# HGRN output transposed in the third gate product's slot, v transposed beside the diagonal, and four other reorderings in a one-core decoder step

## The chip, the cores and the metric

The kernel runs on one core of one Trainium2 chip (trn2). The metric is the time of one launch in microseconds of device time: 2454.43 us in the median of three runs (2454.26 to 2455.49). The engines are TensorE (PE, matmuls; PEld is its weight load), VectorE (DVE), ScalarE (ACT), GpSimd (POOL) and SyncE (SP, which only issues DMAs).

## The reference, cut to what matters

One decoder layer over 2096 tokens of width 1024: 16 meta tokens and 2048 prompt tokens as one sequence, and 8 running sequences of 4 tokens ("the tail").

```python
u = rmsnorm(x) @ w_in                      # 1024 -> 3072: xa, ga, q, f, i (=v), gb
# RG-LRU group, 4 blocks of 128 channels
xc = conv4(xa);  r = sigmoid(xc @ w_ra);  ig = sigmoid(xc @ w_rx)
a  = exp(-8 * r * softplus(-lam));  h = scan(a, sqrt(1 - a*a) * ig * xc)
y_a = h * gelu(ga)
# HGRN2 group, 4 heads of 128 keys x 128 values, in chunks
f = lb + (1 - lb) * sigmoid(f);  k = (1 - lb) * sigmoid(-f_pre);  q = silu(q) / sqrt(128)
o = (q * decay) @ S + tril(q k^T with decay) @ v;   S = S * decay + (k * decay)^T @ v
o = rms(o) * gn * silu(gb)
x = x + concat(y_a, o) @ w_out
x = x + relu(rmsnorm(x) @ w_up)**2 @ w_down          # 1024 -> 4096 -> 1024
y = rmsnorm(x) * ln_final
```

The outputs are y and the states after the last token. All is fp32.

## The kernel before

Activations lie transposed (channels on partitions, tokens along the free axis). The tokens are worked on in two passes: p = 0 has 1024 tokens in two tiles of 512, p = 1 has the other 1072 (the tail among them) in three tiles of 358, 358 and 356. Every dense product is made of three matmuls: weights and activations are each split into a rounded part (`w_hi`, `a_hi`, made by ACT) and a remainder (`w_lo`, `a_lo`), and hi*hi, hi*lo and lo*hi are summed in PSUM (L476 to L478). A unit is one block of 128 output channels for one tile: 8 k-blocks by 3, so 24 matmuls into one of four PSUM banks. There are 96 weight blocks: 24 of the input projection, 8 of the output projection (from `OUT0` = 24), 64 of the MLP. Pass 0 rounds them, makes the remainders and writes both to HBM (`kept_hi`, `kept_lo`); pass 1 only reads them back (`reload`, on POOL's queue), a block when the block two before is done.

The remainder `w_lo` of a weight block is made by `split`. Of pass 0's blocks POOL does 0 and 1, DVE 2 to 23, and POOL all from 24 on.

The order around the change is written out by hand in `schedule(p)`. The input projection has four iterations of five blocks (V, G, XA, F, Q for head i and for RG-LRU block i) and a fifth with the four GA blocks. A block has a slot for each half unit (4 k-blocks, 12 matmuls): 20 slots in an iteration of pass 0, 30 in one of pass 1. All engines walk the same list. Behind the half unit of a slot, PE does the pieces that the list has there; each other engine does its share of the unit (after the second half) and then its share of the pieces, in program order. The pieces of head i-1 run in iteration i: VT (PE transposes v, 9 tiles in pass 1), D (q k^T of 32x32 diagonal blocks), L1 to L7 (the levels above), KT, U (state updates), O (the output), R and N (its norm: DVE inverts the roots, ACT scales), OT (PE transposes the scaled output), Y (DVE multiplies by the gate). GATE(i) is the RG-LRU gate products of block i (4 or 6 matmuls, ACT's sigmoids behind them); GA and GB are the rest of RG-LRU, GB with the scan. Four further PSUM banks (`aux`) are handed round in the list's order; who opens one waits for the reader of the one four before.

Two waits of DVE matter below. It writes v of a new head over the old one:

```python
if kind == V and it > 0:
    filled(dve, AUX[(p, "VT", it - 1)] + 1 + p)
```

that is, `read_out` of a V unit waits until PE has transposed the last tile of the head before. And DVE does GB of block i-1 behind the first V unit (slot 0 in pass 0, slot 1 in pass 1), and in D it multiplies q by f (L1197), on which L1 waits on PE.

The output projection begins with `SIDE` = 4 units side by side, each first for the six k-blocks that are ready early (`EARLY`), then for the last two. Pass 0's final norm is worked in pass 1's first iteration: NF (PE sums squares), FN (DVE's reciprocals), FY (eight scalings and stores). At the end of pass 1 the last two output blocks are taken tile by tile (`FINAL_ORDER`), so that the final norm of a tile (sum on PE, root on ACT, reciprocal and eight scalings on DVE in `finish_tile`, stores on SP) can begin before the last unit.

Of the kernel before, what the change touches and what calls it, by code (L numbers as in the profile page):

```python
# [31 lines left out]
KB = DM // P  # L32
# [27 lines left out]
GA0, OUT0, MLP0 = 20, 24, 32  # L60
OUT_ORDER = [0, 1, 2, 4, 5, 6, 7, 3]
EARLY = 6
SIDE = 4


PC = {}
# [18 lines left out]
def y_no(p, t, n):  # L85
# [4 lines left out]

FINAL_ORDER = [[(m, t) for m in range(KB) for t in range(NT[0])],
               [(m, t) for m in range(KB - 2) for t in range(NT[1])]
               + [(m, t) for t in range(NT[1]) for m in (KB - 2, KB - 1)]]
FINAL_AT = [{mt: n for n, mt in enumerate(order)} for order in FINAL_ORDER]


# [34 lines left out]
def s_at(p, i, name):  # L131
# [3 lines left out]

PREP_STEPS = 25
PIECES = ["VT", "D"] + [f"L{l}" for l in range(1, 8)] + ["KT", "U", "O", "R", "N", "OT", "Y"]
SLOTS = [dict(zip(range(16), PIECES)),
         dict(zip([0, 4, 5, 6, 8, 9, 10, 12, 13, 14, 15, 16, 18, 19, 21, 22], PIECES))]
GATE_SLOT = [16, 24]  # L140
GATE_A_SLOT, GATE_B_SLOT = [18, 27], [0, 1]

SQUARES_AFTER = {1: [0], 2: [1], 3: [2], 4: [3], 5: [4, 5], 6: [6, 7]}
RS_SLOT = [7, 1]

FINAL_SLOTS = {6: ("NF", 0), 7: ("FN", 0), 8: ("FN", 1), **{10 + b: ("FY", b) for b in range(8)}}
TURN_SLOTS = [{14: 0}, {20: 0, 22: 1}]


def schedule(p):  # L150

    out = []
    for i in range(HEADS + 1):
        blks = [5 * i + b for b in range(5)] if i < HEADS else [GA0 + c for c in range(4)]
        s = 0
        for blk in blks:
            for t in range(NT[p]):
                for half in range(2):
                    pieces = []
                    if p and i == 0 and s in FINAL_SLOTS:  # L160
                        pieces.append(FINAL_SLOTS[s])
                    if i == 0 and s == RS_SLOT[p]:
                        pieces.append(("RS", 0))
                    if i >= 1 and s in SLOTS[p]:
                        pieces.append((SLOTS[p][s], i - 1))
                    if i < HEADS and s == GATE_SLOT[p]:
                        pieces.append(("GATE", i))
                    if i < HEADS and s == GATE_A_SLOT[p]:
                        pieces.append(("GA", i))
                    if i >= 1 and s == GATE_B_SLOT[p]:  # L170
# [41 lines left out]
def build(nc, ins, outs):  # L212
# [6 lines left out]
    with ExitStack() as ctx:  # L219
# [200 lines left out]
        @block.gpsimd  # L420
        def _(pool):
            pool.memset(ones[:, :], 1.0).then_inc(consts, 1)
            pool.memset(eps[:, :], EPS).then_inc(consts, 1)
            pool.memset(hprev[:, :], 0.0).then_inc(consts, 1)
            pool.memset(xhist[:, :, :], 0.0).then_inc(consts, 1)
            pool.memset(state[:, :, :], 0.0).then_inc(consts, 1)

            def split(slot, n):

                pool.wait_ge(w_split, n + 1)  # L430
                pool.tensor_tensor(w_lo[:, slot, :], w_st[:, slot, :], w_hi[:, slot, :].bitcast(F32),  # L431
                                   ALU.subtract).then_inc(w_ready, 1)

            pool.wait_ge(consts, 1)
            for j in range(2):
                split(j, j)
            pool.wait_ge(w_ready, OUT0)
            with pool.Fori(OUT0 // 2, BLOCKS // 2) as i:
                for j in range(2):
                    split(j, 2 * i + j)  # L440

            def reload(m, slot):
                pool.dma_start(w_hi[:, slot, :], kept_hi[m]).then_inc(w_again[slot], 16)  # L443
                pool.dma_start(w_lo[:, slot, :], kept_lo[m]).then_inc(w_again[slot], 16)

            pool.wait_ge(w_ready, BLOCKS)
            pool.memset(q_seq[:, :, :], 0.0).then_inc(q_spread, 1)
            for j in range(2):
                pool.wait_ge(w_kept[j], 32 * (BLOCKS // 2))
                pool.wait_ge(unit_done, unit_no(0, BLOCKS + j - 1, 0))  # L450
                reload(j, j)
            with pool.Fori(1, BLOCKS // 2) as i:
                for j in range(2):
                    pool.wait_ge(unit_done, 2 * NT[1] * i + unit_no(1, j - 1, 0))
                    reload(2 * i + j, j)
# [3 lines left out]
        def _(pe):  # L459
# [165 lines left out]
            for p in range(2):  # L625
# [18 lines left out]
                             y_ready if m == 0 else None, lambda j: y_no(p, t, j))  # L644

                units = [(m, t) for m in range(KB) for t in range(nt)]
                for m, t in units[:SIDE]:
                    if t == 0:
                        weights(p, OUT0 + m)
                    open_unit(unit_no(p, OUT0 + m, t))  # L650
                    out_unit(m, t, range(EARLY))
                for m, t in units[:SIDE]:
                    out_unit(m, t, range(EARLY, KB))
                for m, t in units[SIDE:]:
                    if t == 0:
                        weights(p, OUT0 + m)
                    open_unit(unit_no(p, OUT0 + m, t))
# [54 lines left out]
            for m, t in FINAL_ORDER[1][-2 * NT[1]:]:  # L712
# [1 line left out]
                    mlp_weights(last, 1, 1, m - 4)  # L714
                unit = mlp_unit(last, 1, 1, m - 4, t, FINAL_AT[1][(m, t)] - 4 * NT[1])
                products(*unit, halves(0))
                if t and m == KB - 2:
                    final_sum(1, t - 1)
                products(*unit, halves(1))
            final_sum(1, NT[1] - 1)  # L720

# [2 lines left out]
        def _(act):  # L724
# [94 lines left out]
            def piece(p, name, i):  # L819
# [50 lines left out]
                elif name == "O":  # L870
# [9 lines left out]
                    if p:  # L880
                        fn(o_ss[0:T8, 8:9], o_ss[0:T8, 8:9], ACT.Sqrt, bias=eps[0:T8, 0:1], scale=1.0 / P)
                    fn(o_ss[:, 0:NCH], o_ss[:, 0:NCH], ACT.Sqrt, bias=eps[:, 0:1],
                       scale=1.0 / P).then_inc(o_sums, 1)
                    if p and i + 1 < HEADS:
                        act.wait_ge(s_step, s_at(p, i, "smul"))
                        load_state(i + 1)
                    if p:
                        for s in (3, 4):
                            drained(act, AUX[(p, "U", i)] + s)
                        act.dma_start(ssn_d[i], tmp[:, :, :]).then_inc(s_store, 16)  # L890
                elif name == "N":
# [64 lines left out]
            for p in range(2):  # L956
# [42 lines left out]
                    drained(act, AUX[(1, "U", 3)] + 2)  # L999
                    act.dma_start(sp_d, state[:, :, :]).then_inc(small_out, 16)  # L1000

                turn(p, NT[p] - 1, range(EARLY))
                if p == 0:
                    round_weights(OUT0 + 1)
                for t in range(NT[p]):
                    turn(p, t, range(EARLY, KB))

# [55 lines left out]
                for m, t in FINAL_ORDER[p]:  # L1063
# [11 lines left out]
                    if p == 0 and (m, t) == (KB - 1, 0):  # L1075
                        act.wait_ge(unit_done, unit_no(0, BLOCKS - 1, 0) + 1)
                        round_x(1, 0)
                    if p and t and m == KB - 2:
                        rms_tile(1, AUX[(1, "NF", 0)], rf, t - 1, KEPT)
            rms_tile(1, AUX[(1, "NF", 0)], rf, NT[1] - 1, KEPT)  # L1080

            act.wait_ge(s_store, 16 * HEADS)
# [4 lines left out]
        def _(dve):  # L1087
# [310 lines left out]
            for p in range(2):  # L1398
# [13 lines left out]
                queue = []  # L1412
                started = False
                for it, blk, t, half, pieces in schedule(p):
                    if p == 0 and 0 < blk < OUT0 - 1 and t == 0 and half == 0:
                        n = blk + 1
                        dve.wait_ge(w_ready, n)
                        dve.wait_ge(w_split, n + 1)
# [111 lines left out]

            for m, t in FINAL_ORDER[1]:
                last_sum(m, t)
                if t and m == KB - 2:
                    finish_tile(t - 1, range(3))
                elif t and m == KB - 1:
                    finish_tile(t - 1, range(3, KB))
            finish_tile(NT[1] - 1, range(KB))


# [92 lines left out]
```

## Time and profile before

| | us |
|---|---|
| median of the runs | 2454.43 |
| the profiled execution's own time | 2457.05 |
| its span | 2455.2 |
| PE busy | 2393.2 |
| DVE, ACT, POOL busy | 940.7, 643.8, 287.6 |
| mean granted clock of TensorE | 0.989 |

Times in rows are microseconds from the span's start. In the view of the instructions in order of time a row has start, length, engine, line, operation, out<-in, and in brackets the idle time of that engine just before and what ended it. In the table by stretches the fields behind the colon are the stretch's length, busy time and count of instructions for each engine, the granted clock of TensorE (1.00 is 2.4 GHz, 0.50 is 1.2 GHz), the DMA engines' share and GB/s.

### The profile page before, as it was taken

Reading aid. Unit: us, or ns where it says so; the run is one execution under the profiler, and the core shown is the slowest. Engines: PE = TensorE matmul, PEld = TensorE weight load, DVE = VectorE, ACT = ScalarE, POOL = GpSimd, SP = SyncE. Lnnn points to the kernel's source line nnn. Section 1 sums busy time; section 2 is a strip of 40 time slices with the busy share of each in tenths; the row PEclk is TensorE's granted clock in tenths of the full one; section 3 lists DMA queues with packets and bytes.
Section 4 is the critical chain, followed back from the end, with each engine's and each line's share of the span. In section 5 each row is a group of like instructions: output and inputs, shape, how many; then the busy total and the mean of one; then the engine's idle time right before and its main releaser. Section 6 shows DMA issues by size and latency. Waiting matters only on the chain.

```text
span 2455.2 us, 38591 instructions
## 1 busy us (share of the span) xinstructions
PE 2393.2 (97%) x15842; PEld 2148.2 (87%) x15842; DVE 940.7 (38%) x1593; ACT 643.8 (26%) x1199; POOL 287.6 (12%) x276
## 2 busy tenths in 40 slices
PE   7999998999999999999999999999999999999997
PEld 5777786888888888888898899999999999999996
DVE  6766564421121121223765566544212211211224
ACT  5345343331131121223334234422201201200211
POOL 0000002222122122222000000010000100000000
PEclk9999998999999999999999999999999999999998
DMA  5332325444444434454422222332222232223223
GB/s 199 108 114 97 109 91 176 137 156 143 151 133 149 153 130 153 144 201 145 138 96 69 70 70 87 98 136 91 90 86 86 88 100 86 85 85 93 95 86 106
DMA packets 88162, 284.39 MB, mean 116 GB/s; under 512 B 15856, under 2 KB 19056, under 8 KB 88048
## 3 DMA queue, kind: packets, MB, share of 16 engines
q1 hardware_dynamic: 46512, 158.09, 19.0%
q0 software_dynamic: 27648, 100.68, 12.7%
q10 hardware_dynamic: 13888, 23.95, 2.9%
q8 instruction: 90, 1.47, 0.2%
q14 instruction: 24, 0.20, 0.0%
HBM read 171.07 MB, written 111.62 MB: 115 GB/s over the span
## 4 chain that ended last, share of the span: by engine, by line
PE 88%; DVE 6%; issue 3%; ACT 2%; ACTq 1%; DMA 0%; POOL 0%; DVEq 0%; POOLq 0%
PE bank L476 28%; PE bank L478 27%; PE bank L477 27%; PE aux L617 1%; PE aux L543 1%; DVE a_lo L1178 1%; DVE xc L1361 1%; PE aux L571 1%; ACT s_in L726 1%; PE aux L594 1%; PE aux L593 1%; PE aux L548 0%; DVE xy L1287 0%; DVE rs L1122 0%; DVE xy L1113 0%
## 5 line engine op out<-in xcount | busy, mean ns | idle before, releaser
L476 PE MATMUL bank<-a_hi,w_hi 128*128 128x358 f32 (+3 forms) x2560 | 923.8, 361 | 31.1 <-DVE a_lo L1178 11.4
L477 PE MATMUL bank<-a_lo,w_hi 128*128 128x358 f32 (+3 forms) x2560 | 906.7, 354 | 0.0
L478 PE MATMUL bank<-a_hi,w_lo 128*128 128x358 f32 (+3 forms) x2560 | 906.6, 354 | 0.0
L476 PEld LDWEIGHTS bank<-a_hi,w_hi 128*128 128x128 f32 x2560 | 485.8, 190 | 82.6 <-POOL w_lo L431 19.3
L478 PEld LDWEIGHTS bank<-a_hi,w_lo 128*128 128x128 f32 x2560 | 486.5, 190 | 43.6
L477 PEld LDWEIGHTS bank<-a_lo,w_hi 128*128 128x128 f32 x2560 | 486.4, 190 | 42.9 <-issue 1.5
L476 PE MATMUL bank<-b_hi,w_hi 128*128 128x358 f32 (+3 forms) x1280 | 450.2, 352 | 0.0
L477 PE MATMUL bank<-b_lo,w_hi 128*128 128x358 f32 (+3 forms) x1280 | 449.1, 351 | 0.0
L478 PE MATMUL bank<-b_hi,w_lo 128*128 128x358 f32 (+3 forms) x1280 | 449.1, 351 | 0.0
L1489 DVE TENSOR_TENSOR xy<-xy,bank 128x356 f32 (+6 forms) x160 | 94.1, 588 | 554.9 <-PE bank L478 554.9
L726 ACT ACTIVATE a_hi<-tmp 128x356 f32 (+5 forms) x160 | 88.3, 552 | 817.3 <-DVE tmp L1479 817.3
L431 POOL TENSOR_TENSOR w_lo<-w_st,w_hi 128x1024 fp32r<-128x1024 f32 x74 | 183.8, 2484 | 975.4 <-ACT w_hi L726 975.4
L478 PEld LDWEIGHTS bank<-b_hi,w_lo 128*128 128x128 f32 x1280 | 240.8, 188 | 20.6
L477 PEld LDWEIGHTS bank<-b_lo,w_hi 128*128 128x128 f32 x1280 | 240.4, 188 | 20.7 <-issue 0.2
L476 PEld LDWEIGHTS bank<-b_hi,w_hi 128*128 128x128 f32 x1280 | 240.2, 188 | 19.9 <-issue 0.2
L1479 DVE SCALAR_TENSOR_TENSOR tmp<-bank,rs 128x356 f32<-128x356 f32 (+2 forms) x160 | 94.6, 591 | 332.1 <-PE bank L478 331.1
L443 POOL DMA_DIRECT2D w_hi<-kept_hi x96 | 51.2, 534 | 1144.1 <-PE bank L478 1144.1
L726 ACT ACTIVATE w_hi<-w_st 128x1024 fp32r<-128x1024 f32 x96 | 100.9, 1051 | 276.0 <-PE bank L478 272.9
L1482 DVE TENSOR_TENSOR a_lo<-tmp,a_hi 128x356 f32 (+5 forms) x160 | 95.2, 595 | 197.9 <-ACT tmp L726 197.9
L726 ACT ACTIVATE tmp<-tmp 128x356 f32<-128x356 f32 (+2 forms) x160 | 85.7, 535 | 0.0
L726 ACT ACTIVATE tmp<-xy 128x496 f32<-128x496 f32 (+2 forms) x75 | 40.8, 545 | 146.2 <-DVE xy L1489 146.2
L726 ACT ACT_TABLE_LOAD x57 | 73.1, 1283 | 6.9 <-issue 5.9
(162 smaller groups left out, 1417.3 us busy)
## 6 DMA issues: line engine op xcount, KB each, us to landing
w_st<-in_wall SPq DMA_DIRECT2D x96, 512.0 KB, 4.1
kept_hi<-w_hi SPq DMA_DIRECT2D x96, 512.0 KB, 4.9
kept_lo<-w_lo SPq DMA_DIRECT2D x96, 512.0 KB, 5.7
w_hi<-kept_hi POOLq DMA_DIRECT2D x96, 512.0 KB, 4.0
w_lo<-kept_lo POOLq DMA_DIRECT2D x96, 512.0 KB, 4.7
xs<-in_xT ACTq DMA_DIRECT2D x8, 536.0 KB, 7.5
xy<-in_xT ACTq DMA_DIRECT2D x8, 536.0 KB, 8.3
xy<-in_xT ACTq DMA_DIRECT2D x8, 512.0 KB, 7.7
```

The costliest lines, as they stand in the source:

```text
L431: pool.tensor_tensor(w_lo[:, slot, :], w_st[:, slot, :], w_hi[:, slot, :].bitcast(F32), ALU.subtract).then_inc(w_ready, 1)
L443: pool.dma_start(w_hi[:, slot, :], kept_hi[m]).then_inc(w_again[slot], 16)
L476: pe.matmul(ps, wh, xh, start=(j == 0), stop=False)
L477: pe.matmul(ps, wh, xl, start=False, stop=False)
L478: mm = pe.matmul(ps, wl, xh, start=False, stop=(j == 7))
L543: mm = pe.matmul(ps[s0:s0 + w, HALF * c:HALF * (c + 1)], k[:, at:at + w], right_halves(q, at, w, x), start=True, stop=True)
L571: mm = pe.matmul(ps[:, j * P:(j + 1) * P], k_tok[0:r_, c + j, :], v_tok[0:r_, c + j, :], start=True, stop=True)
L593: pe.matmul(out, q[:, lo_:hi_], s_in[:, c + j, :], start=True, stop=False)
L726: return nc.scalar.activation(out, in_, func, **kw)
L1479: stt(z, bank[lu % 4][:, 0:w], 0.0, rs[:, c0:c0 + w], ALU.max, ALU.mult).then_inc(bank_free[lu % 4], 1)
L1482: tt(a_lo[:, 4 * qd + j, c0:c0 + w], z, a_hi[:, 4 * qd + j, c0:c0 + w].bitcast(F32), ALU.subtract).then_inc(h_ready, 1)
L1489: tt(x, x, bank[lu % 4][:, 0:w], ALU.add).then_inc(bank_free[lu % 4], 1)
```

## The change

Nothing is computed otherwise; order and engines change.

1. `AT`: the slots of the pieces. VT goes from slot 0 to slot 1 in pass 0 and from slot 0 to slot 4 in pass 1, so that it stands right ahead of D. GATE(i) goes one slot ahead (16 to 15, 24 to 23), and OT and Y of head i-1 go into that slot, ahead of it. In the fifth iteration (`AT_LAST`, no GATE) OT and Y keep slots 14 and 15 in pass 0 and get 22 and 23 in pass 1.
2. FN, FY and NF of pass 0 go three slots back (NF from slot 6 to 9, FN to 10 and 11, FY to 13 to 20).
3. The remainders of blocks 2, 3 and 4 are made by POOL and no longer by DVE (`DVE_FIRST` = 5).
4. Output projection of pass 0: three units side by side in place of four, and ACT rounds block 25 ahead of the second tile's `turn`, no longer behind it.
5. ACT's load of the next state and its store of the last one go from behind O to behind N.
6. The last six units of pass 1 are reordered, with the sums and `finish_tile`.

```diff
-SIDE = 4
+SIDE = [3, 4]
+DVE_FIRST = 5
@@
-               + [(m, t) for t in range(NT[1]) for m in (KB - 2, KB - 1)]]
+               + [(KB - 2, 0), (KB - 2, 1), (KB - 1, 0), (KB - 1, 1), (KB - 2, 2), (KB - 1, 2)]]
+SUM_AT = {(KB - 1, 1): 0, (KB - 2, 2): 1}
@@
-SLOTS = [dict(zip(range(16), PIECES)),
-         dict(zip([0, 4, 5, 6, 8, 9, 10, 12, 13, 14, 15, 16, 18, 19, 21, 22], PIECES))]
-GATE_SLOT = [16, 24]
+AT = [[1] + list(range(1, 14)) + [15, 15],
+      [4, 4, 5, 6, 8, 9, 10, 12, 13, 14, 15, 16, 18, 19, 23, 23]]
+AT_LAST = [AT[0][:-2] + [14, 15], AT[1][:-2] + [22, 23]]
+GATE_SLOT = [15, 23]
@@
-FINAL_SLOTS = {6: ("NF", 0), 7: ("FN", 0), 8: ("FN", 1), **{10 + b: ("FY", b) for b in range(8)}}
+FINAL_SLOTS = {9: ("NF", 0), 10: ("FN", 0), 11: ("FN", 1), **{13 + b: ("FY", b) for b in range(8)}}
@@ schedule
-                    if i >= 1 and s in SLOTS[p]:
-                        pieces.append((SLOTS[p][s], i - 1))
+                    if i >= 1:
+                        at = (AT if i < HEADS else AT_LAST)[p]
+                        pieces += [(name, i - 1) for name, slot in zip(PIECES, at) if slot == s]
@@ gpsimd
-            for j in range(2):
-                split(j, j)
+            for n in range(DVE_FIRST):
+                split(n % 2, n)
@@ tensor
-                for m, t in units[:SIDE]:
+                for m, t in units[:SIDE[p]]:
...
-                if t and m == KB - 2:
-                    final_sum(1, t - 1)
+                if (m, t) in SUM_AT:
+                    final_sum(1, SUM_AT[(m, t)])
@@ scalar: "O" -> behind "N"
-                    if p and i + 1 < HEADS:
-                        act.wait_ge(s_step, s_at(p, i, "smul"))
-                        load_state(i + 1)
-                    if p:
-                        for s in (3, 4):
-                            drained(act, AUX[(p, "U", i)] + s)
-                        act.dma_start(ssn_d[i], tmp[:, :, :]).then_inc(s_store, 16)
...
-                turn(p, NT[p] - 1, range(EARLY))
                 if p == 0:
                     round_weights(OUT0 + 1)
+                turn(p, NT[p] - 1, range(EARLY))
@@ vector
-                    if p == 0 and 0 < blk < OUT0 - 1 and t == 0 and half == 0:
+                    if p == 0 and DVE_FIRST - 1 <= blk < OUT0 - 1 and t == 0 and half == 0:
...
-                if t and m == KB - 2:
-                    finish_tile(t - 1, range(3))
-                elif t and m == KB - 1:
-                    finish_tile(t - 1, range(3, KB))
+                if (m, t) == (KB - 1, 1):
+                    finish_tile(0, range(5))
+                elif (m, t) == (KB - 2, 2):
+                    finish_tile(0, range(5, KB))
+            finish_tile(1, range(KB))
             finish_tile(NT[1] - 1, range(KB))
```

## Rows read from the trace of the kernel before

**Rows 1.** The page: busy time and share of each engine.
```profile
PE 2393.2 (97%) x15842; PEld 2148.2 (87%) x15842; DVE 940.7 (38%) x1593; ACT 643.8 (26%) x1199; POOL 287.6 (12%) x276
```
**Rows 2.** The table by stretches, two of dense products, one in each pass.
```profile
500.00:525.00 25.00, 25.00 (x112) 20.70 (x111) 6.16 (x9) 8.54 (x13) 5.82 (x3) 1.00 0.53 183
...
2000.00:2300.00 300.00, 300.00 (x1837) 300.00 (x1836) 60.38 (x114) 33.49 (x75) 26.45 (x50) 1.00 0.28 90
```
**Rows 3.** The same table, behind three waits of PE.
```profile
407.00:413.00 6.00, 5.68 (x14) 4.59 (x15) 3.33 (x5) 2.19 (x3) 1.99 (x2) 0.50 0.73 249
...
1314.00:1321.00 7.00, 6.62 (x26) 5.96 (x24) 1.68 (x3) 1.67 (x6) 0.00 (x0) 0.52 0.01 2
...
1492.00:1499.00 7.00, 6.62 (x42) 6.16 (x42) 2.80 (x6) 2.39 (x9) 0.52 (x1) 1.00 0.00 0
```
**Rows 4.** Instructions in order of time, DVE, pass 1, iteration 1, slots 1 to 4.
```profile
1253.77 0.53 DVE L1321 TENSOR_TENSOR v<-bank,rs 128x358 f32<-128x358 f32 x1 [1.17 <-PE bank L478]
...
1260.32 1.28 DVE L1197 TENSOR_TENSOR q<-q,f 128x1072 f32<-128x1072 f32 x1 [0.42 <-PE aux L530]
```
**Rows 5.** The same view, PE: where D and L1 begin.
```profile
1259.48 0.31 PE L530 MATMUL aux<-q,k 128*32 128x32 f32 x13
...
1262.33 0.45 PE L543 MATMUL aux<-q,k 128*32 128x16 f32 x32
```
**Rows 6.** Chain that ended last: start, length, what; N on ACT, GATE on PE.
```profile
1312.51 2.17 ACT s_in L726 x8
...
1324.46 3.60 PE aux L617 x12
```
**Rows 7.** Instructions in order of time: OT on PE, Y on DVE.
```profile
1313.69 0.33 PE L608 MATMUL aux<-ident,s_in 128*128 128x128 f32 x1 [1.96 <-ACT s_in L726]
...
1314.45 0.75 DVE L1263 SCALAR_TENSOR_TENSOR xy<-aux,par,gate 128x512 f32<-128x512 f32 x1 [0.77 <-PE aux L608]
```
**Rows 8.** The same view, output projection of pass 0: ACT, DVE, POOL, PE.
```profile
376.28 3.22 ACT L726 ACTIVATE a_hi<-xy 128x512 fp32r<-128x512 f32 x6
...
378.33 6.07 DVE L1170 TENSOR_TENSOR a_lo<-xy,a_hi 128x512 fp32r<-128x512 f32 x10
...
399.33 0.67 DVE L1459 TENSOR_TENSOR xy<-xy,bank 128x496 f32<-128x496 f32 x1 [14.93 <-PE bank L478]
...
380.52 6.07 POOL L431 TENSOR_TENSOR w_lo<-w_st,w_hi 128x1024 fp32r<-128x1024 f32 x1 [12.43 <-ACT w_hi L726]
...
386.65 0.78 PE L476 MATMUL bank<-a_hi,w_hi 128*128 128x496 f32 x1 [3.08 <-POOL w_lo L431]
...
407.32 0.78 PE L476 MATMUL bank<-a_hi,w_hi 128*128 128x496 f32 x1 [4.00 <-POOL w_lo L431]
```
**Rows 9.** The same view, start of pass 1: NF's second sum on PE, DVE's first reciprocal.
```profile
1196.49 2.04 PE L493 MATMUL aux<-gate,ones 128*128 128x512 f32 x2 [4.77 <-ACT rs L726]
...
1197.48 2.39 DVE L1103 RECIPROCAL rs<-rs 128x358 f32<-128x358 f32 x1 [10.04 <-DMA spad<-in_conv]
```
**Rows 10.** The same view, pass 0: DVE beside POOL, and iteration 0.
```profile
406.55 1.25 DVE L1461 SCALAR_TENSOR_TENSOR b_lo<-xy,par,b_hi 128x496 fp32r<-128x496 f32 x1 [1.28 <-ACT tmp L726]
...
69.92 1.28 DVE L1321 TENSOR_TENSOR f<-bank,rs 128x512 f32<-128x512 f32 x2
...
79.36 0.69 DVE L1321 TENSOR_TENSOR q<-bank,rs 128x512 f32<-128x512 f32 x1 [4.25 <-PE bank L478]
...
70.06 0.50 PE L476 MATMUL bank<-a_hi,w_hi 128*128 128x512 f32 x1 [2.00 <-DVE w_lo L1419]
...
248.00 0.28 PE L543 MATMUL aux<-q,k 128*32 128x16 f32 x11 [0.62 <-DVE q L1197]
```
**Rows 11.** The same view, the end: the last weight, DVE's last sum and scalings.
```profile
2416.41 0.43 PE L476 MATMUL bank<-a_hi,w_hi 128*128 128x358 f32 x1 [3.60 <-DMA w_lo<-kept_lo]
...
2443.33 0.53 DVE L1512 TENSOR_TENSOR gate<-gate,tmp 128x356 f32<-128x356 f32 x1 [0.56 <-ACT tmp L726]
...
2448.70 4.09 DVE L1113 SCALAR_TENSOR_TENSOR xy<-xy,par,gate 128x356 f32<-128x356 f32 x8
```

More of the change, by code:

```diff
@@ L651, in _ @@
                     out_unit(m, t, range(EARLY))
-                for m, t in units[:SIDE]:
+                for m, t in units[:SIDE[p]]:
                     out_unit(m, t, range(EARLY, KB))
-                for m, t in units[SIDE:]:
+                for m, t in units[SIDE[p]:]:
                     if t == 0:
@@ L899, in piece @@
                         ins.then_inc(aux_free[(ao + s) % 4], 1)
+                    if p and i + 1 < HEADS:
+                        act.wait_ge(s_step, s_at(p, i, "smul"))
+                        load_state(i + 1)
+                    if p:
+                        for s in (3, 4):
+                            drained(act, AUX[(p, "U", i)] + s)
+                        act.dma_start(ssn_d[i], tmp[:, :, :]).then_inc(s_store, 16)
                 elif name == "TURN":
@@ L1077, in _ @@
                         round_x(1, 0)
-                    if p and t and m == KB - 2:
-                        rms_tile(1, AUX[(1, "NF", 0)], rf, t - 1, KEPT)
+                    if p and (m, t) in SUM_AT:
+                        rms_tile(1, AUX[(1, "NF", 0)], rf, SUM_AT[(m, t)], KEPT)
             rms_tile(1, AUX[(1, "NF", 0)], rf, NT[1] - 1, KEPT)
```

## The prediction

> **What bounds the kernel now.** The page comes first: PE is busy 97% of the span, DVE 38% [rows 1]. So an edit counts only by what it does to PE's idle time and clock, and to the tail behind PE's last product. The table by stretches gives PE's pace: 0.223 us a product in pass 0 (25 us by 112), 0.163 in pass 1 (300 by 1837) [rows 2]; a half unit of 12 is 2.7 and 1.96 us, a unit twice that. Then the waits of PE in the order of time [rows 7 to 11]: 2.00 at 70 us, 3.08 and 4.00 in the output projection of pass 0, 4.77 at the start of pass 1, 1.96 for OT, 3.60 for the last weight. Last the same table behind such waits [rows 3]: the clock is at 0.50 (the 1.2 GHz level) for the 6 us behind the wait of 4.00, at 0.52 for 7 us behind that of 1.96, and at 1.00 behind the same OT wait two heads later. So a drop costs about half of its 6 to 7 us, 3 us, and a wait near 2 us may or may not bring it. I take 2.7 for a drop where part of it passes in the wait itself.
>
> All sums are made on the profiled execution: 2457.05 us, span 2455.2, which is 2.6 over the median of the runs (2454.43). I carry the difference over to the median.
>
> **VT beside D in pass 1: a new wait, +14.4 and +8.1 us.** PE's own work ahead of L1 is the same in both orders. But DVE's first V read of a new head, in slot 1, waits for VT of the old one, and VT is now behind slot 4. Queued behind that read on DVE are GB with its scan, the second V read, then q times f in D, and PE waits for that in L1. The row of q times f and that of the first V read give the length of this queue: 1260.32 - 1253.77 less 0.42 idle is 6.1 us, and 1.28 for the product, 7.4 us [rows 4]. VT's last tile is done about when D began, 1259.48, and some 0.3 us pass until DVE sees it: 1259.8 + 7.4 = 1267.2 in place of 1262.33 [rows 5], so 4.8 us. Nothing hides it: PE has D alone and one half unit (2.0 us) between VT and L1. It comes in iterations 1, 2 and 3 (the fifth reads no V): 14.4 us. Each of these waits is longer than the 4.00 us one that brought the clock down [rows 3, 8], so three drops of 2.7, 8.1 us. Bounds: no drops at 14.4, three full ones at 24.9. In pass 0 VT goes back one slot only and DVE reaches that V read later than VT ends: nothing.
>
> **OT and GATE in one slot, pass 1: -9.9 us.** ACT's scaling N of eight tiles begins at 1312.51 and lasts 2.2 us [rows 6]; PE stands 1.96 us for its first tiles [rows 7]. Two half units later (3.9 us) N is over. From the half unit ahead of OT (1311.7, where the idle 1.96 begins) to the first product behind GATE (1324.46 + 3.60 = 1328.1, less 0.4 overlap: 1327.6 [rows 6]) it was 15.9 us with a drop. Anew: three half units 5.9, OT 1.1, GATE 3.4, and a new wait inside. GATE's second product needs the aux bank that Y of OT's first four tiles frees, and DVE is still at the last F tile and the three steps of the one before, about 1.9 us from the slot's end, then Y with 0.75 [rows 7]: PE stands 0.9. Sum 11.3 with 0.2 of changes between kinds of product: 4.4 less. Heads 0 and 1 alike; head 2 had no drop [rows 3]: 1.4. Together 10.2; ACT's two DMA issues now stand in front of the last F tile, so I take 9.9. Bounds: 5 if OT, the new wait and GATE bring a drop of their own, 11.
>
> **The same in pass 0: -0.2 us.** OT's wait goes there too (about 0.9 us a head), but L1 waits for DVE's q times f, idle 0.62 [rows 10], and DVE's chain to it begins with a remainder that now waits until ACT is through with GATE. PE is earlier by 0.8 and DVE by 0.05, so PE waits longer at L1. Bounds: -2.5 and +1.5.
>
> **Remainders 2 to 4 on POOL: +2.2 and +2.3 us.** DVE is spared three products of about 1.23. The first lets the reciprocals start 0.6 earlier, worth 0.3 at the low clock. The third falls on the convolution of block 0. A DVE step with two SBUF inputs beside POOL's product takes 1.25 us in place of 0.73 [rows 10]: it stands until POOL is done. POOL's product is 2.4 us, so the first two-input tap ends 2.1 us late, DVE reads F at 70.5 and no longer at 69.92, and behind it ACT does F, now GATE too (five steps and a table load, 6 us), and only then rounds block 5, whose remainder stands ahead of DVE's read of Q: 81.6 for 79.36 [rows 10]. L1 follows by the same 2.2. PE no longer waits 2.00 at 70.06 [rows 10], does GATE one slot sooner, and so stands 3.7 us more at L1: a drop, 2.7 with a chance of 0.85, 2.3. Bounds: -1 (DVE is not held) and +6.
>
> The Trainium skill has a rule on this, in GPSIMD Engine Reference, section Key points: the engine shares its SBUF interfaces with VectorE and contends with instructions in a two-port mode or with two SBUF inputs. The trace agrees (1.25 for 0.73, and POOL's own product 6.07 us beside a run of such steps [rows 8]); without that rule the edit would be a gain of about 1 us.
>
> **Output projection of pass 0: -12.0 us.** Block 25 is rounded at 376.3, where `turn` began, and no longer behind it [rows 8]; POOL's product starts at 377.4, ahead of DVE's run of a_lo at 378.33, and ends at 379.8 where it was 386.6. The run is held to 380.3: PE waits 1.6 at the second tile. Three early parts end at 388.5 (18 products each), the late parts of the first two at 389.9 and 391.2, of the third at 392.6; then unit (1,1) with 24 products to 398.2. The first unit's end leads to remainder 26: before, 399.33 (DVE's read) to 407.3 [rows 8], 8.0 us; now 390.1 to 398.1. So (2,0) starts at 398.2 where it was 407.32: 9.1. The drop behind 407 goes, 2.9 [rows 3]. Bounds: -8.5 if POOL loses to DVE as at 380.52, -12.5.
>
> **Start of pass 1: +4.9 us.** PE's wait at NF, 4.77, hid NF and one half unit under a wait that stays: unit 4 needs the bank of the first V tile, read by DVE at 1197.48 + 2.39 + 0.53 = 1200.4, and that start hangs on a small DMA [rows 4, 9]. With NF three slots later PE runs dry at 1192.7, goes on at 1200.5 and does NF's 1.8 us in the open: 2.5 us late by slot 10, the low clock taken alike. Then the scalings FY stand behind the convolution, three of 1.2 us more than before, so the last F tile is read at 1238.7 while GATE starts at 1235.8; its fifth product waits for ACT's first sigmoid, 2.1 us. With 0.3 of shifts 4.9. Bounds: 1 and 7.
>
> **The end: -2.9 us.** With (6,1) between (6,0) and (7,0) the last weight has a unit more to land: the wait of 3.60 and its low clock go. But of tile 1 all stays for the end. Behind DVE's last sum (2443.33) were five scalings, a reciprocal and eight (2448.70 + 4.09) [rows 11]: 9.5 us. Now two reciprocals of 2.39 [rows 9] and sixteen scalings of 0.51, 13.0, behind a last sum at 2436.9 (PE is done at 2434.3, DVE has three scalings of tile 0 ahead): 2449.9. Bounds: -4.5 and 0.
>
> **Small ones: -0.4 us,** for four joined stretches of transposes in pass 1. ACT's later DMAs have room (the state is needed a head later).
>
> Sum: 14.4 + 8.1 - 9.9 - 0.2 + 4.5 - 12.0 + 4.9 - 2.9 - 0.4 = +6.5. 2457.05 + 6.5 = 2463.5 for the profiled kind of execution, and 2460.9 for the median.
>
> **The rivals.** (a) The waits are there but bring no new drops: -8.1 - 2.3, so 2450.5. For it: 1.00 behind the third OT wait [rows 3]; against it, these waits are twice as long. (b) The wait for VT doesn't reach PE, since DVE's queue behind V is shorter than PE's work to L1 or is made up later: -22.5, 2438. Against it: 7.4 us stand against 2.9. This is the way in which the change would plainly gain. (c) POOL starves in the output projection as at 380.52 and the gain there is 8.5: 2464.4. (d) OT, the wait for Y and GATE together bring a drop in each of three heads: +8, 2469. [...]
>
> **How the numbers follow.** A measurement of this kernel tells some 0.2% (4.9 us) from no change. Forecast 0.55, with its own range 2456 to 2466; (a) 0.14; (b) 0.06; (c) 0.14; (d) 0.11. Faster: (b) and a quarter of (a), with a little for gains that I priced low, 0.12. Slower, above 2459.3: seven tenths of the forecast, most of (c) and all of (d), 0.63. Within: 0.25. The range takes (a) and (d): 2449 to 2470.
>
> **What would show it.** In pass 1, iterations 1 to 3: PE idle 4.8 us ahead of L1 (L543), released by L1197, clock 0.5 behind it, and the first V read beginning behind L520. OT (L608) with no wait; 0.9 ahead of GATE's second product. Pass 0: (2,0) some 9 us earlier against its stage's start, POOL's product of block 25 at 2.4 us; a tap of the convolution at 3.4 us or so where it was 1.28; L1 at 97.7. Pass 1: NF with no wait, an idle time of 7.8 us ahead of slot 8. The end: thirteen us from the last sum to the last scaling. If L1's wait in pass 1 is below 3 us, or no drop follows, the forecast is wrong in its sign.

## The result, and the profile after

The changed kernel takes 2458.85 us in the median of 20 runs (2457.79 to 2461.25), the kernel before 2455.18 in 20 runs beside them (2453.61 to 2458.73): a ratio of 1.0015 [1.0009, 1.0021], 3.7 us slower (2.2 to 5.2 by the interval), where 6.5 were forecast. That is less than the 4.9 us which the forecast gave as the least that a measurement tells from no change; with 20 runs of each kernel it is clear of the noise. The profiled execution took 2460.49, its span is 2458.3 (before: 2457.05 and 2455.2), the mean granted clock 0.989 in both. Line numbers behind L422 are four higher than before.

The page says nothing of where the time went: each engine is as busy as in [rows 1].

```profile
PE 2387.6 (97%) x15842; PEld 2145.5 (87%) x15842; DVE 939.7 (38%) x1590; ACT 646.0 (26%) x1201; POOL 291.6 (12%) x279
```

The waits of PE by what ended them do (total us, times, longest).

```profile
PE aux L547 <- DVE q L1201: 21.2, 7, 4.5
PE bank L480 <- DVE v L1325: 13.5, 2, 7.9
...
PE aux L621 <- ACT ta L730: 1.4, 1, 1.4
PE aux L621 <- DVE xy L1267: 1.3, 3, 0.4
```

The first row is L1 waiting for q times f: seven waits with 21.2 us. The wait of OT (L612) is gone in pass 1, and three of 0.4 for Y stand inside GATE (L621). What answers to [rows 4] and [rows 5], on PE and on DVE, in order of time:

```profile
1265.74 1.05 PE L547 MATMUL aux<-q,k 128*32 128x16 f32 x64 [4.54 <-DVE q L1201]
```
```profile
1258.38 0.53 DVE L1325 TENSOR_TENSOR v<-bank,rs 128x358 f32<-128x358 f32 x1 [6.99 <-PE aux L524]
1258.83 1.26 DVE L1282 TENSOR_TENSOR k_tok<-k_tok,ea 128x1072 f32<-128x1072 f32 x1
...
1260.68 2.45 DVE L1291 TENSOR_TENSOR_SCAN xy<-ta,hprev,k_tok 128x1072 f32<-128x1072 f32 x1
...
1263.97 0.53 DVE L1325 TENSOR_TENSOR v<-bank,rs 128x358 f32<-128x358 f32 x1
1264.42 1.27 DVE L1201 TENSOR_TENSOR q<-q,f 128x1072 f32<-128x1072 f32 x1
```

DVE stands 6.99 us for VT (L524), then does its whole queue, and q times f ends at 1265.7, when L1 starts. From the start of the V read it is 7.3 us, where I had 7.4. The table by stretches shows the clock behind the three such waits (to be read as [rows 3]):

```profile
1263.70:1270.50 6.80, 4.76 (x80) 4.52 (x80) 5.64 (x14) 0.00 (x0) 0.00 (x0) 0.50 0.37 127
...
1355.80:1362.70 6.90, 6.00 (x148) 5.56 (x148) 4.57 (x11) 0.00 (x0) 0.00 (x0) 0.51 0.21 77
1448.00:1451.40 3.40, 3.33 (x76) 3.29 (x76) 3.17 (x9) 0.00 (x0) 0.00 (x0) 0.50 0.15 53
```

Two times the 1.2 GHz level lasts 6.8 us, the third time 3.4, behind waits of one length (4.54, 4.55, 4.54). OT, the wait for Y and GATE in one slot, PE, against [rows 6] and [rows 7]:

```profile
1320.95 1.22 PE L612 MATMUL aux<-ident,s_in 128*128 128x128 f32 x9
1322.10 0.87 PE L621 MATMUL aux<-xc,w_ra 128*128 128x358 f32 x2
1323.39 0.87 PE L621 MATMUL aux<-xc,w_rx 128*128 128x358 f32 x2 [0.42 <-DVE xy L1267]
```

Behind them the clock stays at 1.00. Elsewhere, also in order of time: in pass 0 the first tap of the convolution beside POOL's product of block 4, and iteration 1's L1; in the output projection POOL's product of block 25 and PE's wait; the start of pass 1 on PE; the end on DVE.

```profile
57.97 2.87 POOL L435 TENSOR_TENSOR w_lo<-w_st,w_hi 128x1024 fp32r<-128x1024 f32 x1 [6.16 <-ACT w_hi L730]
...
58.60 4.64 DVE L1365 SCALAR_TENSOR_TENSOR xc<-xpad,par,xc 128x1024 f32<-128x1024 f32 x2
...
80.33 1.22 DVE L1423 TENSOR_TENSOR w_lo<-w_st,w_hi 128x1024 fp32r<-128x1024 f32 x1 [6.59 <-ACT w_hi L730]
...
97.60 1.06 PE L547 MATMUL aux<-q,k 128*32 128x16 f32 x64 [3.52 <-DVE q L1201]
...
382.44 2.38 POOL L435 TENSOR_TENSOR w_lo<-w_st,w_hi 128x1024 fp32r<-128x1024 f32 x1 [9.30 <-ACT w_hi L730]
...
385.51 0.47 PE L480 MATMUL bank<-a_hi,w_hi 128*128 128x512 f32 x1 [2.03 <-DVE a_lo L1174]
...
1195.85 0.67 PE L480 MATMUL bank<-a_hi,w_hi 128*128 128x358 f32 x1 [7.92 <-DVE v L1325]
...
1234.29 0.87 PE L621 MATMUL aux<-xc,w_ra 128*128 128x356 f32 x2 [1.35 <-ACT ta L730]
...
2442.51 0.53 DVE L1516 TENSOR_TENSOR gate<-gate,tmp 128x356 f32<-128x356 f32 x1 [0.57 <-ACT tmp L730]
...
2451.80 4.09 DVE L1117 SCALAR_TENSOR_TENSOR xy<-xy,par,gate 128x356 f32<-128x356 f32 x8
```

The same event of PE in both traces, one under the other, gives what each stage cost. "Forecast" is the term of the prediction.

| stretch, to the event | before | after | stage | forecast |
|---|---|---|---|---|
| pass 0 to OT of iteration 4 | 370.05 | 375.09 | +5.0 | +4.3 |
| to the MLP's norm sums, pass 0 | 480.82 | 475.90 | -10.0 | -12.0 |
| to slot 25 of pass 1, iteration 0 | 1238.49 | 1237.3 | +3.7 | +4.9 |
| three times V read, VT, D, L1 | | | +13.8, and +5.9 by the clock | +14.4, +8.1 |
| three times OT, Y, GATE | | | -11.5 | -9.9 |
| to the norm sums of pass 1 | 1680.89 | 1687.49 | -0.4 | -0.4 |
| to the end of the span | 2455.2 | 2458.3 | -3.5 | -2.9 |

For the pass 1 rows, L1 of iteration 1 moves from 1262.33 to 1265.74, of iteration 2 from 1351.43 to 1356.70, of 3 from 1440.61 to 1448.07, and slot 25 of the three iterations from 1327.63, 1416.77, 1502.97 to 1328.26, 1419.65, 1509.94. (In the changed kernel slot 25 is taken as the end of GATE and one half unit of 1.98 us.) From slot 25 to the next L1 it takes 4.6 us more each time, which is the wait. From L1 to slot 25 it takes 2.8, 2.4 and 0.5 less, and that holds two things, the low clock and OT with GATE. Experiment 1 separates them: it has the same list from L1 on, and its clock isn't low there. From L1 to OT it takes 53.17, 53.18 and 53.18 us, the changed kernel 55.21, 55.64 and 54.56. So the low clock costs 2.0, 2.5 and 1.4 us, and OT with GATE gives 4.8, 4.9 and 1.9.

### The profile page after: what moved, and what is told of

Same layout as the page of the kernel before. It is cut to its first block, busy times and chain, and to the rows that moved or that the text cites. A ratio compares the mean times of both kernels' runs of the same rounds, so it can differ in the third digit from the quotient of the medians.

```text
span 2458.3 us, 38591 instructions
## 1 busy us (share of the span) xinstructions
PE 2387.6 (97%) x15842; PEld 2145.5 (87%) x15842; DVE 939.7 (38%) x1590; ACT 646.0 (26%) x1201; POOL 291.6 (12%) x279
## 4 chain that ended last, share of the span: by engine, by line
PE 88%; DVE 6%; ACT 2%; issue 1%; DMA 1%; ACTq 0%; DVEq 0%; POOL 0%; POOLq 0%
PE bank L480 28%; PE bank L482 27%; PE bank L481 27%; PE aux L547 1%; PE aux L621 1%; DVE xy L1291 1%; DVE xy L1117 1%; PE aux L575 1%; PE aux L598 1%; PE aux L597 1%; PE aux L552 1%; DVE a_lo L1182 0%; ACT L730 0%; DVE q L1201 0%; DVE k_tok L1282 0%
```

## Experiments

Runs of the kernel before beside them had medians of 2454.90 us (9 runs, experiments 1 to 4), 2455.89 (21 runs, 5 to 8) and 2455.74 (11 runs, 9 to 11). Two edits have no run of their own: VT one slot later in pass 0, and ACT's two DMAs behind N.

**1. VT back in slot 0 in pass 1.** The changed kernel with one number changed.

```diff
-      [4, 4, 5, 6, 8, 9, 10, 12, 13, 14, 15, 16, 18, 19, 23, 23]]
+      [0, 4, 5, 6, 8, 9, 10, 12, 13, 14, 15, 16, 18, 19, 23, 23]]
```

> The changed kernel with one number put back: VT of pass 1 in slot 0 again (D stays in 4). Theory (DVE's V read waits for VT, GB and q times f are queued behind it): the three waits of PE ahead of L1 (4.6, 4.6 and 4.6 us in the trace of the changed kernel) and the three low-clock stretches behind them (some 2.4, 3.0 and 1.7) go: 20.8 us less than the changed kernel, about 2438, clock 1.00 through iterations 1 to 3 of pass 1. Rival 1: the low clock there comes from the stretch of small products and stays: 13.8 less, 2445. Rival 2: what PE waits for is GB itself, wherever VT stands, since GATE is now a slot sooner: less than 5 us gained, above 2453.

2439.86 us (2437.65 to 2442.03), 0.9938 [0.9924, 0.9952]: 19.0 us below the changed kernel, near the 20.8 of the theory. The V read and L1's product on DVE, and PE's waits:

```profile
1250.20 0.53 DVE L1325 TENSOR_TENSOR v<-bank,rs 128x358 f32<-128x358 f32 x1 [1.15 <-PE bank L482]
...
1256.73 1.28 DVE L1201 TENSOR_TENSOR q<-q,f 128x1072 f32<-128x1072 f32 x1 [0.41 <-PE aux L534]
```
```profile
PE aux L547 <- DVE q L1201: 7.7, 4, 3.5
```
```profile
1250.00:1540.00 290.00, 288.71 (x3402) 267.84 (x3401) 187.18 (x386) 104.09 (x242) 18.57 (x34) 1.00 0.23 74
```

The V read now waits for its own bank and q times f for D; the four waits left are pass 0's, and the clock is at 1.00 through iterations 1 to 3. So one slot number decides the change's sign.

**2. VT in slot 4 alone**, in the kernel before.

```diff
-                    if i >= 1 and s in SLOTS[p]:
+                    if p and i >= 1:
+                        pieces += [(name, i - 1) for name in PIECES if AT1[name] == s]
+                    elif i >= 1 and s in SLOTS[p]:
```
(`AT1` is the old list of pass 1 with VT at 4.)

> The kernel before with VT of pass 1 in slot 4 beside D, and nothing else of the change. Theory: three waits of 4.6 to 4.8 us ahead of L1 and a drop of the clock behind each (1.7 to 3.4 us): 20 to 24 us over before, 2475 to 2479. Rival 1 (the drops depend on the rest of the change): +14, 2469. Rival 2 (the wait only exists with GATE in slot 23): within 3 us of before.

2473.48 us (2471.97 to 2475.62), 1.0073 [1.006, 1.0087]: some 18 us, a little under what was expected.

```profile
1266.43 1.05 PE L547 MATMUL aux<-q,k 128*32 128x16 f32 x64 [4.55 <-DVE q L1201]
```
```profile
1264.90:1271.70 6.80, 5.27 (x104) 4.83 (x108) 5.20 (x12) 0.00 (x0) 0.00 (x0) 0.56 0.28 102
```

The three waits (4.55, 4.53, 4.55) make 13.6. The low clock behind them costs 2.6, 1.5 and 2.2 us, read from L1 to OT of each head against the kernel before. But in this execution the clock was low for only 3.4 us behind the waits of OT in heads 0 and 1, and for 6.8 in the kernel before [rows 3]: from OT to GATE it takes 1.8 and 1.0 us less. That is why the sum stays below 20.

**3. OT, Y and GATE in slot 23 alone**, in the kernel before.

```diff
-GATE_SLOT = [16, 24]
+GATE_SLOT = [16, 23]
...
+AT1 = [dict(zip(PIECES, [0, 4, 5, 6, 8, 9, 10, 12, 13, 14, 15, 16, 18, 19] + ends)) for ends in ([23, 23], [21, 22])]
```

> The kernel before with OT and Y of pass 1 in slot 23 together with GATE (from 21, 22 and 24) in iterations 1 to 3, GATE in 23 in iteration 0 too, and nothing else of the change. Theory: OT's waits (2.0 us, three times) go, a wait of 0.6 inside GATE comes, the two drops behind OT at 1314 and 1403 go, and iteration 0 loses about 1 at GATE's fifth product, where ACT is still at the last F tile: 11.6 less than before, 2443.6. Rival 1: the two drops come anyway, from transposes and gate products side by side: 5 less, 2450. Rival 2: what was won at OT is given back at GATE's wait for Y: within 2 us.

2444.7 us (2442.9 to 2447.21), 0.9957 [0.9943, 0.997]. No wait at OT, 0.42 inside GATE, no low clock in either head:

```profile
1315.47 1.23 PE L611 MATMUL aux<-ident,s_in 128*128 128x128 f32 x9
...
1317.92 0.87 PE L620 MATMUL aux<-xc,w_rx 128*128 128x358 f32 x2 [0.42 <-DVE xy L1266]
```
```profile
1280.00:1370.00 90.00, 89.58 (x993) 82.79 (x992) 56.67 (x116) 34.35 (x81) 5.68 (x11) 1.00 0.25 83
```

**4. Final norm of pass 0 in its old slots**, on top of experiment 1.

```diff
-FINAL_SLOTS = {9: ("NF", 0), 10: ("FN", 0), 11: ("FN", 1), **{13 + b: ("FY", b) for b in range(8)}}
+FINAL_SLOTS = {6: ("NF", 0), 7: ("FN", 0), 8: ("FN", 1), **{10 + b: ("FY", b) for b in range(8)}}
```

> As the first, and FINAL_SLOTS as before the change too (NF in slot 6, FN in 7 and 8, FY in 10 to 17). Theory (NF and one half unit are hidden by a wait that stays; behind slot 8 NF stands in the open, and FY behind the convolution makes GATE's fifth product wait): 2.5 to 3.7 less than the first kernel, 2434.5 to 2435.5. Rival: the cost at the start of pass 1 is that of GATE one slot sooner, and NF's place is worth nothing: the same as the first kernel, 2438.

2438.11 us (2437.49 to 2438.49), 1.75 below experiment 1, less than was expected and not apart from it by the intervals (0.9931 [0.9917, 0.9945] for 0.9938 [0.9924, 0.9952]); in the trace the stretch from the residual's sums to VT of iteration 1 (1172.68 to 1245.61) is 2.4 shorter (1171.66 to 1246.99 there). NF's wait is back and hides its own work, but a wait inside iteration 0's GATE stays:

```profile
1190.08 2.05 PE L497 MATMUL aux<-gate,ones 128*128 128x512 f32 x2 [4.80 <-ACT rs L730]
...
1230.56 0.86 PE L621 MATMUL aux<-xc,w_ra 128*128 128x356 f32 x2 [1.57 <-ACT ta L730]
```

With FY in its old slots GATE still starts 2.2 us ahead of DVE's read of the last F tile (1226.42 and 1228.62). Experiment 3 has the old slots too and stands 1.38 us at the same place. So this wait comes from GATE in slot 23, not from FY; experiment 11 takes it away.

**5. Remainders 2 to 4 back on DVE**, on top of experiment 1.

```diff
-DVE_FIRST = 5
+DVE_FIRST = 2
```

> The first kernel (VT of pass 1 in slot 0) with the remainders 2 to 4 on DVE again (DVE_FIRST = 2), GATE still in slot 15 of pass 0. Theory (POOL's product holds the first two-input tap of the convolution for 2.1 us, and the three products that DVE is spared are worth less): the tap takes 1.28 us, not 3.32, PE waits 2.0 for remainder 4 at 70 us again, L1 of iteration 1 begins 0.5 to 1 sooner than 97.6 and with 1 to 2 us of idle ahead of it in place of 3.5, so that the drop there goes: 2 to 4 less than the first kernel, 2436 to 2438. Rival 1 (POOL's help is worth its place, the late L1 comes from GATE alone): 1 to 2 more, 2441. Rival 2: what counts is the order on ACT and both are alike within 0.5.

2438.1 us (2436.68 to 2439.39), 0.9929 [0.9916, 0.9943]. The reason given for it fell. The hold is gone (three taps in 3.92 us), yet DVE does its own product instead, and F is read at 70.08, 0.1 sooner than in experiment 1 counted from PE's start (43.42 here, 42.78 there, F at 69.57). L1 is as late as before, with the same wait:

```profile
59.02 3.92 DVE L1365 SCALAR_TENSOR_TENSOR xc<-xpad,par,xc 128x1024 f32<-128x1024 f32 x3
...
68.94 1.23 DVE L1423 TENSOR_TENSOR w_lo<-w_st,w_hi 128x1024 fp32r<-128x1024 f32 x1
...
97.12 1.06 PE L547 MATMUL aux<-q,k 128*32 128x16 f32 x64 [3.54 <-DVE q L1201]
```

By the medians it is 1.8 us below experiment 1, again inside the intervals. So what makes L1 late is not where the remainders are made. The row of 80.33 in the changed kernel names it: DVE stood 6.59 us for ACT's rounding of block 5, and that is behind GATE's sigmoids. Experiments 8 and 10 take that up.

**6. ACT rounds block 25 ahead of the second tile's turn, alone**, in the kernel before.

```diff
-                turn(p, NT[p] - 1, range(EARLY))
                 if p == 0:
                     round_weights(OUT0 + 1)
+                turn(p, NT[p] - 1, range(EARLY))
```

> The kernel before with ACT's rounding of block 25 ahead of the second tile's turn, nothing else (four units side by side). Theory: POOL's product takes 2.4 in place of 6.07 and PE's wait of 3.08 at (1,0) falls to 0, the wait for a_lo grows from 0.7 to 2; the wait of 4.0 ahead of (2,0) stays, since remainder 26 hangs on the first unit's end: 2 to 5 less than before (a drop may go), 2450 to 2453. Rival (the order on ACT is all of the gain): 10 less, 2445.

2451.89 us (2450.73 to 2453.8), 0.9986 [0.9977, 0.9995].

```profile
377.69 2.38 POOL L431 TENSOR_TENSOR w_lo<-w_st,w_hi 128x1024 fp32r<-128x1024 f32 x1 [9.30 <-ACT w_hi L726]
...
380.77 0.47 PE L476 MATMUL bank<-a_hi,w_hi 128*128 128x512 f32 x1 [2.04 <-DVE a_lo L1170]
...
404.42 0.78 PE L476 MATMUL bank<-a_hi,w_hi 128*128 128x496 f32 x1 [4.00 <-POOL w_lo L431]
```

POOL's product is 2.38 us and not 6.07, but DVE's run of a_lo is held behind it, so PE waits 2.04 there; the wait of 4.00 stays.

**7. The end's order alone**, in the kernel before.

```diff
-               + [(m, t) for t in range(NT[1]) for m in (KB - 2, KB - 1)]]
+               + [(KB - 2, 0), (KB - 2, 1), (KB - 1, 0), (KB - 1, 1), (KB - 2, 2), (KB - 1, 2)]]
+SUM_AT = {(KB - 1, 1): 0, (KB - 2, 2): 1}
```

> The kernel before with the new order of the last six units, their sums and finish_tile, nothing else. Theory (3.6 of waiting for the last weight and its low clock go, 3.5 more of DVE work stand behind the last sum): 3 to 3.5 less than before, 2451.5. Rival 1 (the weight's wait was made up by DVE's backlog anyway): 0. Rival 2 (DVE's longer tail gives all back): 1 more.

2452.11 us (2450.09 to 2454.95), 0.9984 [0.9975, 0.9993]: 1.7 to 6.1 us by the interval, 3.8 by the medians, where the forecast's term was 2.9. The weight's wait of 3.60 [rows 11] is gone from the waits of PE.

**8. GATE in slot 16 in pass 0, OT and Y ahead of it in 15, remainder 4 on DVE**, on top of experiment 4.

```diff
-GATE_SLOT = [15, 23]
+GATE_SLOT = [16, 23]
-DVE_FIRST = 5
+DVE_FIRST = 4
```

> VT of pass 1 in slot 0, FINAL_SLOTS as before the change, and in pass 0 GATE in slot 16 again with OT and Y still in 15; POOL makes remainders 2 and 3, DVE 4. Theory (in pass 0 the gain at OT was given back at L1, since ACT's rounding for the next block, and with it DVE's remainder and its read of Q, stood behind GATE): L1 of iteration 1 near 95.2 in place of 97.6 and no drop (-4 to -5), the idle time ahead of L1 in the later iterations 0.6 and not 1.4, the period of an iteration 75.2 and not 76.1 (-2.5): 6 to 7 less than the kernel with VT and FINAL_SLOTS put back, 2431 to 2432. Rival (L1's wait in pass 0 is set by GB's scan whatever ACT does): period 76.1, only the first 4: 2434.

2428.08 us (2426.96 to 2429.51), 0.9887 [0.9872, 0.9902], better than was expected and 10.0 below experiment 4. ACT rounds block 5 at 72.26, ahead of GATE's sigmoids; in the changed kernel it does so at 79.19, behind them. L1 comes at 95.08 with an idle 0.55, and from iteration 2 to 4 it takes PE 75.04 and 75.00 us a head, where the changed kernel and the one before both need 76.0 to 76.1. What stays is

```profile
69.58 0.53 PE L480 MATMUL bank<-a_hi,w_hi 128*128 128x512 f32 x1 [1.99 <-DVE w_lo L1423]
...
95.08 0.74 PE L547 MATMUL aux<-q,k 128*32 128x16 f32 x64 [0.55 <-DVE q L1201]
...
1221.74 1.16 PE L621 MATMUL aux<-xc,w_ra 128*128 128x356 f32 x2 [1.96 <-ACT ta L730]
```
```profile
1222.20:1225.60 3.40, 3.40 (x10) 2.66 (x9) 0.00 (x0) 2.75 (x5) 0.00 (x0) 0.50 0.31 112
```

**9. Three units side by side alone**, in the kernel before.

```diff
-SIDE = 4
+SIDE = [3, 4]
```

> The kernel before with three units side by side in pass 0's output projection in place of four, and nothing else; ACT still rounds block 25 behind the second tile's turn. The change as a whole gained 10.0 us there, the rounding's order alone 3.3 (2451.9). Theory (the two gains stand apart and add up): POOL's product of block 25 is still 6.07 us and PE still waits 3.1 for it near 386.7, but the first unit is finished 4 us sooner, so the wait of 4.00 for remainder 26 and the low clock behind it (2.9) go: about 6.9 less, 2448 to 2449. Rival (the gain needs both, since the product of block 25 holds up remainder 26 too): the wait behind it stays at 2 or more, with a drop, and the time is 2453 or above.

2448.44 us (2443.25 to 2451.47), 0.9966 [0.9955, 0.9977]. POOL's product is 6.07 us still and PE waits 3.08 for it; at (2,0), where PE waited 4.00 for remainder 26, it goes on without an idle time. POOL and PE, in order of time; the last row is the first product of (2,0):

```profile
381.38 6.07 POOL L431 TENSOR_TENSOR w_lo<-w_st,w_hi 128x1024 fp32r<-128x1024 f32 x1 [12.42 <-ACT w_hi L726]
...
387.51 0.78 PE L476 MATMUL bank<-a_hi,w_hi 128*128 128x496 f32 x1 [3.08 <-POOL w_lo L431]
...
404.05 0.50 PE L476 MATMUL bank<-a_hi,w_hi 128*128 128x496 f32 x1
```

So the two edits of that stage add up: 3.4 and 8.3 us by the ratios, each with some 2.5 either way, against 10.0 in the changed kernel's trace.

**10. As 8, with remainder 4 on POOL.**

```diff
-DVE_FIRST = 4
+DVE_FIRST = 5
```

> The fastest version so far (the changed kernel with VT in slot 0 in pass 1, NF, FN and FY of pass 0 in their old slots, GATE in slot 16 in pass 0 with OT and Y in 15, remainder 4 on DVE: 2428.1 us), with the one difference that POOL makes remainder 4 too, over the convolution of block 0, as in the changed kernel. Theory (what made L1 late in pass 0 was GATE ahead of the rounding of block 5, and POOL's hold on a tap costs about what DVE's own product of 1.23 us would): L1 at about 95 in iteration 1 as with remainder 4 on DVE, F read at 70.6 or sooner, no wait of 2 us at 70, time within 1 us of 2428 (or 2 below it, if the wait near 70 was worth its length). Rival (the price that I gave for POOL's hold is real, 2.2 us and more for a drop): L1 at 97 or later with an idle time near 3, and 2430 to 2433.

2431.24 us (2430.62 to 2432.14), 0.9902 [0.9886, 0.9917]. Neither theory holds whole. The tap is held as in the changed kernel, PE doesn't wait near 70, and L1 comes 1.5 us sooner than in experiment 8, not later; but it waits 2.15 there, and the clock falls:

```profile
57.60 4.64 DVE L1365 SCALAR_TENSOR_TENSOR xc<-xpad,par,xc 128x1024 f32<-128x1024 f32 x2
...
75.85 0.69 DVE L1325 TENSOR_TENSOR q<-bank,rs 128x512 f32<-128x512 f32 x1 [1.11 <-PE bank L482]
...
93.61 0.81 PE L547 MATMUL aux<-q,k 128*32 128x16 f32 x64 [2.15 <-DVE q L1201]
```
```profile
94.00:98.00 4.00, 4.00 (x50) 3.21 (x41) 2.34 (x4) 0.00 (x0) 0.00 (x0) 0.57 0.02 9
377.00:381.00 4.00, 4.00 (x11) 3.15 (x12) 4.00 (x8) 1.90 (x4) 0.00 (x0) 0.57 0.85 207
```

Neither stretch is in experiment 8's execution, nor is a third at 1534.5, while its low clock at 1222 isn't here. The first takes most of what L1 had won: at L1 of iteration 2 only 0.2 of the 1.5 us is left (170.37 and 170.58). The profiled spans are 1.1 us apart (2428.8 and 2427.7), the medians 3.2. The mean granted clocks of all the runs point the same way: 0.992 to 0.993 in the four of this experiment, 0.994 to 0.995 in those of experiment 8. A difference of 0.002 over 2430 us is some 5 us by an estimate, rounding aside, so the low clock is enough to account for the 3.2; that nothing else has a part in it isn't shown.

This experiment differs from experiment 4 by GATE's slot in pass 0 alone. L1 comes at 93.61 for 97.19 there, and the time is 6.9 us less by the medians (0.9902 for 0.9931). What is shown is that GATE's slot makes L1 late and POOL's hold doesn't, and that the wait which goes near 70 comes back at L1.

**11. As 8, with GATE of iteration 0 of pass 1 in slot 24.**

```diff
-                    if i < HEADS and s == GATE_SLOT[p]:
+                    if i < HEADS and s == GATE_SLOT[p] + (p == 1 and i == 0):
```

> The fastest version so far (2428.1 us) with one difference: in pass 1, GATE of iteration 0 alone goes back from slot 23 to 24, where DVE and ACT have the scalings FY behind them. Theory (the wait of 1.96 at 1221.7 inside that GATE and the drop of 3.4 us behind it are worth 1.96 and 1.7, and no other wait takes their place, as iteration 0 has no OT): 2424 to 2425.5. Rival (the wait moves on to L1 of iteration 1, because ACT's gates are a slot later): 2427 to 2429.

2426.48 us (2425.78 to 2427.11), 0.9881 [0.9866, 0.9896], the fastest: 29 us below the kernel before, 32 below the changed one. The stage is shorter by what was expected (from the second NF sum to VT of iteration 1 it is 53.4 us, 57.05 in experiment 8), and the clock holds:

```profile
1222.44 0.87 PE L621 MATMUL aux<-xc,w_ra 128*128 128x356 f32 x2
```
```profile
1200.00:1280.00 80.00, 80.00 (x885) 74.70 (x884) 60.27 (x114) 23.22 (x43) 5.29 (x10) 1.00 0.36 119
```

The profiled spans are 3.2 us apart, the medians only 1.6, between the two theories. In this execution the clock fell behind PE's wait of 1.99 near 69 us, where it had not in experiment 8's; and experiment 8's profiled execution was the slowest of its four. The mean granted clocks of the four runs are alike in both (0.994 or 0.995), which fits a gain of the wait of 1.96 alone. But with four runs each 1.6 us is not separated from 3.6 with certainty. No new wait at L1 was found (the four together are 2.3 us, 2.4 in experiment 8).

## Why the prediction was right, and where its sizes were off

The mechanism was right, and the range and the sign. The sum of the table is +5.0 - 10.0 + 3.7 + 13.8 + 5.9 - 11.5 - 0.4 - 3.5 = +3.0, the span says +3.1, the forecast +6.5. Part of that is luck: the terms were too low by 2.7 us together and too high by 6.2, and what was left is 3.5. The median is also below the 2459.3 from which the forecast called it slower (0.63); it fell into the band of no change, which had 0.25.

- **VT beside D, +14.4 and +8.1: shown.** Idle 4.54 at each L1 for 4.8, with DVE's V read behind VT as its releaser; experiment 2 shows it alone (4.55), experiment 1 without (19.0 us). The three drops came, one of them half as long, and cost 5.9 us: 2.7 each was too much.
- **OT and GATE in one slot, -9.9: too small, measured -11.5.** Per head it is 4.8, 4.9 and 1.9 for 4.4, 4.4 and 1.4. The 0.5 of each is the wait for Y, 0.42 where I reckoned 0.9: Y began at 1322.60, which is 0.25 sooner, and GATE's first product lay over more of it. The 0.3 that I took off for ACT's DMAs did not show. No low clock followed in any of the three heads, so rival (d) fell. Experiment 3 alone gives 10.6 us by its ratio [7.4, 14.0]; in its trace it is 11.7 from L1 of iteration 1 to L1 of iteration 4, less the 1.38 of iteration 0.
- **Output projection, -12.0: -10.0.** POOL's product began where I had it (382.44 is the 377.4 of the forecast and the 5.0 of pass 0) and took 2.38 for 6.07. But PE waited 2.03 and not 1.6, and the clock was low behind it for 3.4 us:

```profile
386.40:389.90 3.50, 3.50 (x10) 2.72 (x9) 3.50 (x7) 1.13 (x3) 0.00 (x0) 0.51 0.89 233
```

  I had counted no drop for this wait, though it is as long as that of [rows 7], behind which the clock fell in one head and held in another.
- **Remainders on POOL, +4.5: +5.0, the right time with its cause half wrong.** Each step is in the trace: the tap of 3.3 us (I said 3.4), F at 70.55 (70.5), Q at 81.48 (81.6), L1 at 97.60 (97.7), a drop. But I booked the late rounding of block 5 on the remainders' account, and it is GATE's: with GATE in slot 16 and the same remainders on POOL (experiment 10) Q is read at 75.85 and L1 comes at 93.61. POOL's hold costs about what DVE's own product costs (experiment 5). And the -0.2 for OT and GATE in pass 0 hid a gain of 1 us a head: from iteration 2 on L1 comes every 75.0 us in experiments 8 and 10, every 76.1 with GATE in slot 15.
- **Start of pass 1, +4.9: +3.7.** The idle time behind NF's removal was 7.92 (I said 7.8), that inside GATE 1.35 where I had 2.1. For the second wait I blamed the scalings FY behind the convolution, and that was wrong: it is as long with FY in the old slots (experiments 3 and 4) and goes with GATE in slot 24 (experiment 11).
- **The end, -2.9: -3.5,** with 12.9 us from the last sum to the last scaling (13.0).
- **Rivals.** (a) no drops: fell. (b) the wait does not reach PE: fell; its price of 2438 is nearly what experiment 1 gives by really taking the wait away. (c) POOL starves: fell, 2.38 us.

The Trainium skill states, in SBUF — State Buffer, section Who interferes with whom, that a DVE instruction with two SBUF inputs contends with a GpSimd instruction that reads SBUF, and, in section SBUF: two separate sides, that whichever starts first has the shared ports for its whole instruction while the other is blocked. The trace agrees both ways: POOL began at 57.97 and the tap of 58.60 ended at 61.9, behind POOL's end at 60.84; beside DVE's run of a_lo POOL's product took 6.07 us [rows 8], and started ahead of it 2.38.

## What to carry to other kernels

Before a producer is moved next to its consumer, follow the buffer that it frees: here the move cost PE nothing by itself, but the next head's first write to v stood behind it, and all of that engine's queue behind the write. Price an engine's queue from the waiting instruction to the one that PE needs (7.3 us) against PE's own work up to there (2.9 us); the difference is the stall, and a drop of the clock comes on top where it is long. When several edits meet in one late event, cross them two by two before one of them is blamed: L1 was late by GATE's place on ACT (experiments 4 and 10), and the edit that I blamed did not make it so.

## What the runs showed of the hardware that was not expected

- Behind idle times of one length (4.54, 4.55, 4.54 us) the clock was at 1.2 GHz for 6.8, 6.8 and 3.4 us, which cost 2.0, 2.5 and 1.4; behind idle times of 1.96 to 2.3 it fell in some executions and heads and held in others of the same kernel's stage (behind 2.0 at 377 us in experiment 10, not in 8; behind 1.99 at 69 us in 11, not in 8). It was also low for 3.4 us at 1534.5 in experiment 10 and at 1542.6 in 4, where the longest idle time of PE in the 20 us before was 0.2. So a wait near 2 us has a price only on average, and the single profiles of two versions can differ by 1.7 us a stretch (half of 3.4) for that alone.
- A product of POOL's that began 0.9 us ahead of DVE's run of two-input steps took 2.38 us, and the first step of the run took 1.99 for 0.68. One that began in the run [rows 8] took 6.07, and DVE's run was not longer for it (6.07 for ten steps). It ended at 386.60, 2.2 us behind the run's end at 384.40: it stood not for one step but for all that was left of the run. So which of the two begins first decides which of them pays.
